# Inverse products of the recurrence on 32 weight columns each, in four column groups

## What is computed

```python
def _wkv_scan(S0, decay, k, v, kk, a, r, reverse):
    def step(S, inp):
        w_t, k_t, v_t, kk_t, a_t = inp[:5]
        sa = jnp.einsum('bhvk,bhk->bhv', S, -kk_t)
        S = (S * w_t[:, :, None, :] + sa[..., None] * (kk_t * a_t)[:, :, None, :]
             + v_t[..., None] * k_t[:, :, None, :])
        y = jnp.einsum('bhvk,bhk->bhv', S, inp[5]) if len(inp) == 6 else None
        return S, y
```

## Time and profile before

| | us |
|---|---|
| three runs | 4139.95, 4149.6, 4151.31 |
| their median | 4149.6 |
| the profiled execution | 4161.02 |
| span of its instructions | 4159.2 |
| busy: PE / PEld / DVE / ACT / POOL | 3647.3 / 2723.7 / 1596.8 / 1026.4 / 1071.6 |

### The profile page before, as it was taken

One profiled execution on the slowest core, in us unless ns is written; L12 is line 12 of the kernel. 1 busy time (PEld: TensorE's weight loads), 2 busy tenths in 40 slices (PEclk: granted clock), 3 DMA queues, 4 the chain that ended last, 5 costly groups with the idle time before them and its releaser, 6 DMA issues.

```text
span 4159.2 us, 82553 instructions
## 1 busy us (share of the span) xinstructions
PE 3647.3 (88%) x36422; PEld 2723.7 (65%) x36422; DVE 1596.8 (38%) x2784; ACT 1026.4 (25%) x1591; POOL 1071.6 (26%) x697
## 2 busy tenths in 40 slices
PE   8897788778867889889999989859999999988997
PEld 3354477623325667668888845438888888866885
DVE  3256522311125555533333340205454554433333
ACT  2132232211113134331111021313223322223221
POOL 0002332021113100133232120025554444424441
PEclk9997899889978999999999989979999999989998
DMA  4207053179951100021111113320000000011221
GB/s 168 91 31 301 28 203 121 72 271 369 360 223 36 33 9 1 31 92 65 68 61 61 68 75 121 152 80 3 14 14 13 14 13 13 3 62 61 102 101 41
DMA packets 64593, 379.24 MB, mean 91 GB/s; under 512 B 12906, under 2 KB 12906, under 8 KB 26352
## 3 DMA queue, kind: packets, MB, share of 16 engines
q1 hardware_dynamic: 40032, 291.52, 18.2%
q0 software_dynamic: 20608, 68.82, 4.3%
q10 hardware_dynamic: 3600, 13.63, 0.9%
HBM read 380.21 MB, written 44.04 MB: 102 GB/s over the span
## 4 chain that ended last, share of the span: by engine, by line
PE 54%; DVE 4%; POOL 3%; ACT 2%; issue 1%; DMA 0%; DVEq 0%; ACTq 0%; POOLq 0%
PE psum L461 13%; PE psum L473 8%; PE psum L474 8%; PE psum L475 8%; PE psum L708 3%; PE psum L2768 2%; PE psum L2755 2%; PE psum L727 1%; PE psum L2733 1%; PE psum L3057 1%; PE psum L606 1%; PE psum L558 1%; DVE arena L2928 1%; PE psum L2906 1%; PE psum L2293 1%
## 5 line engine op out<-in xcount | busy, mean ns | idle before, releaser
L461 PE MATMUL psum<-arena 64*64 64x64 f32 (+4 forms) x14024 | 651.4, 239 | 52.4 <-POOL arena L2991 22.5
L461 PEld LDWEIGHTS psum<-arena 64*64 64x64 f32 (+2 forms) x14024 | 525.7, 142 | 147.6 <-issue 111.0
L491 POOL TENSOR_TENSOR ring_low<-ring,slab_high 128x2048 fp32r<-128x2048 f32 x66 | 304.0, 4621 | 639.6 <-ACT slab_high L484 639.6
L473 PE MATMUL psum<-h_high,slab_high 128*128 128x512 f32 (+1 forms) x1056 | 378.3, 358 | 23.2 <-DVE h_low L511 16.5
L474 PE MATMUL psum<-h_low,slab_high 128*128 128x512 f32 (+1 forms) x1056 | 376.7, 357 | 0.0
L475 PE MATMUL psum<-h_high,ring_low 128*128 128x512 f32 (+1 forms) x1056 | 376.3, 356 | 0.0
L461 PE MATMUL psum<-arena,ring 128*128 128x512 f32 (+3 forms) x960 | 355.9, 531 | 5.2 <-DVEq L1222 5.2
L461 PEld LDWEIGHTS psum<-arena,ring 128*128 128x128 f32 (+2 forms) x960 | 178.7, 187 | 181.0 <-issue 167.3
L473 PEld LDWEIGHTS psum<-h_high,slab_high 128*128 128x128 f32 x1056 | 201.4, 191 | 57.5 <-issue 15.0
L899 DVE TENSOR_TENSOR arena<-arena,psum 128x512 f32<-128x512 f32 x66 | 39.5, 599 | 485.0 <-PE psum L475 480.8
L3235 DVE TENSOR_TENSOR arena<-psum,arena 128x384 f32<-128x384 f32 (+1 forms) x320 | 166.8, 528 | 139.4 <-PE psum L461 121.6
(11 more groups left out here) (429 smaller groups left out, 6382.1 us busy)
## 6 DMA issues: line engine op xcount, KB each, us to landing
ring<-in_wall SPq DMA_DIRECT2D x181, 1024.0 KB, 5.1
arena<-in_wall SPq DMA_DIRECT2D x96, 1024.0 KB, 13.0
moe_rows<-arena POOLq DMA_DIRECT2D x2, 6144.0 KB, 61.4
arena<-moe_rows ACTq DMA_DIRECT2D x24, 512.0 KB
moe_out<-arena POOLq DMA_DIRECT2D x24, 512.0 KB, 9.1
arena<-spill POOLq DMA_DIRECT2D x8, 1024.0 KB, 6.5
spill<-arena POOLq DMA_DIRECT2D x2, 3072.0 KB, 17.5
filters<-arena POOLq DMA_DIRECT2D x2, 2048.0 KB, 6.5
```

The source lines that it names most:

```text
L461: last = L.eng.matmul(out, a, b, start=(i == 0), stop=(i == len(pairs) - 1))
L473: L.eng.matmul(out, a_hi, b_hi, start=(i == 0), stop=False)
L491: L.eng.tensor_tensor(m.low[:, n % SLOTS, :], m.ring[:, n % SLOTS, :], m.high_of(n).bitcast(F32), ALU.subtract).then_inc(m.sem("slab_split ...
```

## The change

The three product families of the inverse are cut into products of 32 weight columns. In the inverse and transposed products each product of 64 weight columns becomes two (`q` = 0, 1) with the same 64 rows and the same 32 moving columns, which write 32 partitions each. In the corner products of levels 2 to 16 only the two 32 x 32 blocks on the diagonal of a square are computed, with 32 rows, 32 weight columns and 32 moving columns; VectorE's mask takes the rest. At level 32 the corner is as before. The order within a column block is q outside and p inside, so four products in a row write four different groups of 32 partitions. The number of products doubles where it applies, and no other engine's instructions change.

```diff
@@ inverse_tensor
     for tt in range(TT):
-        for p in range(2):
-            last = L.eng.matmul(in_blocks(ps[64 * p:64 * p + 64, 32 * tt:32 * tt + 32], lv), square(B.tt, hh, tt, p),
-                                side_of(square(B.x, hh, tt, p), lv, d), start=True, stop=True)
+        for q in range(2):
+            for p in range(2):
+                s = slice(64 * p + 32 * q, 64 * p + 32 * q + 32)
+                last = L.eng.matmul(in_blocks(ps[s, 32 * tt:32 * tt + 32], lv), square(B.tt, hh, tt, p)[:, 32 * q:32 * q + 32],
+                                    side_of(square(B.x, hh, tt, p), lv, d), start=True, stop=True)
...
@@ unit_tensor
-            corner.append(squares_tensor(L, hh, lambda *at: [(square(B.nt, *at), square(B.ti, *at))]))
+            if lv < 32:
+                ps = L.next_bank()
+                for bank_free, count in L.bank_frees:
+                    L.eng.wait_ge(bank_free, count)
+                for tt in range(TT):
+                    for q in range(2):
+                        for p in range(2):
+                            c = (TT * hh + tt) * CH + 32 * q
+                            s = slice(64 * p + 32 * q, 64 * p + 32 * q + 32)
+                            last = L.eng.matmul(ps[s, tt * CH + 32 * q:tt * CH + 32 * q + 32], B.nt[s, c:c + 32], B.ti[s, c:c + 32], start=True, stop=True)
+                last.then_inc(L.bank_full, 1)
+                corner.append(L.read_out)
+            else:
+                corner.append(squares_tensor(L, hh, lambda *at: [(square(B.nt, *at), square(B.ti, *at))]))
```

More of the change, by code:

```diff
@@ L2766, in transposed_tensor @@
     for tt in range(TT):
-        for p in range(2):
-            last = L.eng.matmul(in_blocks(ps[64 * p:64 * p + 64, 32 * tt:32 * tt + 32], lv), square(B.x, hh, tt, p),
-                                side_of(square(B.tt, hh, tt, p), lv, 1 - d), start=True, stop=True)
+        for q in range(2):
+            for p in range(2):
+                s = slice(64 * p + 32 * q, 64 * p + 32 * q + 32)
+                last = L.eng.matmul(in_blocks(ps[s, 32 * tt:32 * tt + 32], lv), square(B.x, hh, tt, p)[:, 32 * q:32 * q + 32],
+                                    side_of(square(B.tt, hh, tt, p), lv, 1 - d), start=True, stop=True)
     last.then_inc(L.bank_full, 1)
```

## The result

The kernel after took **4353.4 us** (median of four runs, 4343.5 to 4367.0) against 4147.4 us for the kernel before, run beside it. The ratio is 1.0501, with a 95% interval of 1.0467 to 1.0535: 206 us slower. The forecast was 4102 us, with 4083 to 4128 as its range.

What follows compares the result with a forecast made beforehand. PE was taken to bound the recurrence, paced by weight columns. Eight pairs of units gaining 4.05 + 1.9 us make 48 us, so 4161 becomes 4113, or 4102 us against the median; own range 4083 to 4128, with rivals 4072 to 4157.

Steps and rivals of the forecast that it cites:

- What PE saves is saved: In the recurrence PE is busy 822.77 of 868 us, so its savings count unless another engine stands next in line.
- lower end: Shortest time for a cut block of 48 records, 0.38 us, from L2293 and the recorded weight-load times.
- 10 ns a record: Pace taken for a cut block in the recurrence, making 0.48 us a block and a gain of 0.22 us each.
- upper end: Slowest case for a cut block: 0.96 us at 20 ns a record, set aside; the forecast's range used 0.59 us.
- The terms for the odd and the even unit: Net gains in the recurrence: 4.05 us per odd unit and 1.9 us per even unit, over 8 pairs.
- The switches between forms: In the recurrence, each change of tile shape on PE was to cost 0.09 us; about four open per odd unit, 0.35 us.
- PE's wait for GpSimd: In even units PE's savings behind the scan become a longer wait for GpSimd's L2991, some 2 us.
- Level 16: Sign of being right: this level of the inverse falls from 4.37 to about 3.3 us.
- at today's 29.2 ns: Slow rival, records have their own pace, at 0.70 us more a block: 4390 us; 0.12 for the whole rival.
- 20 ns variant: Same slow rival with records 20 ns apart: each block costs 0.26 us more, 4240 us; 0.12 for the whole rival.
- Pairs of column groups: Rival: column groups overlap only in pairs, block stays 0.70 us, 4153 us; chance 0.14.
- The clock: Rival: granted clock falls behind every scan in the eight odd units, 16 us back, about 4118 us; chance 0.13.

Runs made afterwards that it cites:

- the kernel with half the instructions: Changed kernel with operands of the three cut families replaced by bfloat16 zeros, one load and one matmul per product, inverse not computed: 4112.4 us, ratio 0.9908.
- the inverse products at 2 and 8: Kernel before with only the inverse products cut, and only at levels 2 and 8: 4142.3 us against 4152.9, ratio 0.9978.
- tall corners: Only the corner products cut to 32 weight columns, each with all 64 rows and 64 moving columns, otherwise the kernel before: 4164.6 us, ratio 1.0044.

## Why the prediction was wrong

**The bound.** "What PE saves is saved" held by the busy times. What it did not say is that PE was at the limit of a second resource already: 14.6 ns an instruction in every block, beside a supply of about 14. Nothing on the page of before shows that as a wait (issue had 4 us in the recurrence).

**How long is a block.** The array's part was right: the lower end was 0.38 us, the value taken 0.48, and blocks whose instructions were there take 0.41 to 0.43 (0.64 us at the lower level of the clock, where about 0.7 was foretold). The failed step is the next one, the choice of 10 ns a record for blocks in a row. The upper end was waived because the 20 ns of the earlier trace rows "is explained by the loads and not by the supply of records". That was true of those rows, and said nothing on the supply; it only showed that nothing in the kernel before had asked for more. The burst of eight loads in 50 ns and the 16 records of L2293 in 1.07 us are far less than a packet of 256 instructions, and say nothing on a pace that lasts. Sustained, a matmul record with its load comes every 27 to 30 ns, three times the value taken.

**The sum.** It put the instructions at nothing: "no transfer or register step is added". The change adds 78 transfers of instructions (1.28 MB), and PE's stops for them are about 195 us of the recurrence. The terms for the odd and the even unit (4.05 and 1.9 us) never came to bear, and no run confirms them: the 38 us of the kernel with half the instructions come with lighter operands and a lower clock, and of the 9 us of the inverse products at 2 and 8 only some 4 us can be read in the rows, the rest goes with a higher clock. The switches between forms, put at 0.09 us, are confirmed (0.12 us behind a cut block). (At the upper end the even unit's own terms give 1.0 us and not 0.9, which is 1 us in the sum.) PE's wait for GpSimd (20.6 us) did not grow, since the even units got longer and not shorter. Level 16, foretold to fall from 4.37 to about 3.3 us, takes 7.8 us in the unit shown (from 3361.56 to 3369.39), partly at the lower level of the clock.

**The rivals.** The time given for a supply of records "at today's 29.2 ns" was 4390 us, and that is nearly what happened: a sustained 27 to 30 ns, less what the reserve and the waits cover. The rival named the right resource, and had 0.12 together with its 20 ns variant. That its size is right as well is luck: 29.2 ns is the pace of the 64-column blocks in the array, which nothing ties to the supply. It was wrong in one point, that every block would be slower: some are fast and then PE stops. Pairs of column groups don't bind (8.9 ns a record), except where 64 columns move, in the tall corners. The clock was priced at 16 us, for falls in eight odd units; with the corners cut alone it is about 99 us. In the change itself little of it shows beside the stops.

The Trainium skill ("TensorE: Matmul & The Clock Gate", section "Wait — 56ns, not 53.3ns?") was cited for about 25 ns between starts, and 4320 us by it. The trace disagrees with it as a floor: matmuls with their loads start 8.9 ns apart in supplied blocks. That its time comes near is a coincidence of 25 ns with 27 to 30 ns of supply.

**What would have shown it.** The queue q8 on the page of before: 290 packets. In its recurrence there were 174 in 868 us, and 19,968 instructions are 78 more there, 252 in all. The forecast wanted the recurrence in about 820 us, that is a packet every 3.25 us from end to end. In the recurrence of the kernel before no two packets are closer than 3.30 us, no five gaps in a row average less than 3.85 us, and the median gap is 4.75 us. So the trace of before had never shown the supply that the forecast took for granted. How much it would cost could not be read there: at the 3.74 us of the changed kernel's stalled gaps 252 packets take 942 us, which is 74 us over the 868. The measured recurrence is 205 us over. That the rest comes from a demand in bursts, with slack that can't be carried over, fits the stops but was not tested by itself.

## What to carry to other kernels

Count instructions as a resource of TensorE, beside columns and bytes: a split that halves each product's work doubles them (four for a float32 product), and where it asked for more than one instruction every 14 ns or so, sustained, the engine stopped for its own program. Such a stop is "idle, issue" in the middle of a group with no semaphore, and the instruction queue's packets give the rate. Cut where a wait ahead of the place lets the supply run ahead, don't expect much of it between blocks of another form, and read the granted clock of the stretch beside it: the corners here lost more by it than they saved.

## What the runs showed of the hardware

- TensorE's instructions come in packets of 16 KB, 256 instructions; the changed kernel's stalled gaps between them are 3.74 us in the median (14.6 ns an instruction), and all of its 115 stops of more than 0.7 us end 2.1 to 3.1 us after the start of a packet. The idle time grew by 195 us for 78 packets more.
- It is not the average alone. The kernel with tall corners uses 200 packets in 868 us, one every 4.3 us, and stands still for some 8 us; the changed kernel uses 251 in 1,072, as often, with 199 us of stops, since it asks in bursts.
- Four column groups of 32 weight columns start a matmul every 8.9 ns with 32 moving columns; with 64 moving columns two blocks take 1.56 us, no less than with 64 weight columns (all at a granted clock of 1.00).
- A block of another form behind a cut one takes 0.82 us where it takes 0.70 behind its like.
- The corners alone, two blocks a level, move the granted clock of the recurrence: 0.95 before, 0.84 with 32 rows and 32 moving columns, 0.86 with 64 rows and 32 moving, 0.98 with 64 and 64, all with 32 weight columns. With a PE that is busy all along this costs about 96 us. Executions of one kernel differ too: the kernel before took 4132 us at 0.938 over the span and 4168 us at 0.927.
- A wait on TensorE's queue for something long free cost 104 ns for each instruction added, at a granted clock of 0.64, more than three of the old records.
- Left open: how large the reserve of instructions is, and what sets the time between packets. No run here varied either. Why the granted clock falls with the cut corners is open too.
